# The second block's input: the first norm's tokens are transposed as they are, and the second norm's factor goes on the projections

## The reference

```python
h = _layer_norm(DEEPNORM_ALPHA * h + ffn, ln2_g, ln2_b)      # end of the first block
hn = _rmsnorm(h, attn_norm[0])                               # h * rsqrt(mean(h*h) + EPS) * g
proj = hn @ w_in                                             # lora (c_q, c_kv, k_r), qB, kB, vB
qA = _rmsnorm(c_q, g_q) @ w_uq;  kv = _rmsnorm(c_kv, g_kv) @ w_ukv
oA = mla(qA with rotated q_rope, k_nope with rotated k_r, vA);  oB = dilated(qB, kB, vB)
h = h + concat(oA, oB) @ w_out
```

## Time and profile before

| | |
|---|---|
| median of 3 runs | 1423.23 us (1423.0 to 1424.0) |
| profiled execution, own time | 1423.59 us |
| its span | 1421.4 us |
| mean granted TensorE clock | 0.995 |
| PE busy | 1385.8 us, 97% |
| DVE busy | 698.3 us, 49% |
| ACT busy | 546.9 us, 38% |

### The profile page before, as it was taken

The page is one execution under the profiler, slowest core; times in us unless marked ns, Lnnn a source line. Parts: engine busy times, 40 slices in busy tenths (PEclk is TensorE's granted clock), DMA queues, the critical chain, the costliest instruction groups (busy, mean ns, idle before and its releaser), DMA issues.

```text
span 1421.4 us, 25839 instructions
## 1 busy us (share of the span) xinstructions
PE 1385.8 (97%) x11120; PEld 1132.7 (80%) x11120; DVE 698.3 (49%) x1102; ACT 546.9 (38%) x867; POOL 18.6 (1%) x15
## 2 busy tenths in 40 slices
PE   7999999999999999999999999999999998999998
PEld 5999999979766566656666568889999986899997
DVE  6866896547611111111111157865555667755555
ACT  4555774344211111111111144763344366633343
POOL 0000004000000000000000000000000000000000
PEclk9999999999999999999999999999999999999999
DMA  9534434018899999999999981335444621454420
GB/s 388 237 120 178 178 135 165 15 48 363 330 397 426 424 427 425 424 426 426 425 426 426 426 354 59 131 133 217 178 177 172 255 106 45 171 197 180 177 89 30
DMA packets 31089, 351.99 MB, mean 248 GB/s; under 512 B 3088, under 2 KB 3344, under 8 KB 4880
## 3 DMA queue, kind: packets, MB, share of 16 engines
q1 hardware_dynamic: 30704, 349.24, 61.0%
q10 hardware_dynamic: 288, 1.31, 0.2%
HBM read 349.49 MB, written 1.05 MB: 247 GB/s over the span
## 4 chain that ended last, share of the span: by engine, by line
PE 90%; DVE 5%; ACT 3%; issue 1%; DMA 0%; DVEq 0%; ACTq 0%
PE psum L442 88%; PE psum L548 2%; ACT pages L1269 1%; PE psum L871 1%; DVE slot_lo L1873 1%; DVE tiny L1821 0%; ACT w_hi L1293 0%; DVE pages L2055 0%; DMA pages<-in_x 0%; ACT mix_hi L1293 0%; DVE pages L2492 0%; DVE pages L2540 0%; DVE pages L2538 0%; DVE pages L1843 0%; ACT tiny L1269 0%
## 5 line engine op out<-in xcount | busy, mean ns | idle before, releaser
L442 PE MATMUL psum<-pages 64*64 64x64 f32 (+9 forms) x3184 | 299.5, 305 | 8.9 <-issue 2.7
L442 PEld LDWEIGHTS psum<-pages 128*64 128x64 f32 (+3 forms) x3184 | 215.2, 151 | 78.9 <-issue 43.0
L442 PE MATMUL psum<-ring,pages 128*64 128x256 f32 (+1 forms) x1652 | 223.2, 424 | 0.9 <-ACT pages L1531 0.9
L442 PE MATMUL psum<-x_hi,gu_hi 128*128 128x256 f32 x704 | 199.8, 284 | 0.1
L442 PE MATMUL psum<-x_hi,gu_lo 128*128 128x256 f32 x704 | 199.2, 283 | 0.0
L442 PE MATMUL psum<-x_lo,gu_hi 128*128 128x256 f32 x704 | 199.2, 283 | 0.0
L442 PEld LDWEIGHTS psum<-ring,pages 128*64 128x64 f32 x1652 | 117.1, 137 | 92.1 <-issue 42.6
L442 PEld LDWEIGHTS psum<-x_hi,gu_hi 128*128 128x128 f32 x704 | 134.9, 192 | 2.7 <-issue 0.6
L442 PEld LDWEIGHTS psum<-x_lo,gu_hi 128*128 128x128 f32 x704 | 134.9, 192 | 1.6
L442 PEld LDWEIGHTS psum<-x_hi,gu_lo 128*128 128x128 f32 x704 | 134.9, 192 | 0.0
L1873 DVE TENSOR_TENSOR slot_lo<-ring,mix_hi 128x2048 fp32r<-128x2048 f32 x44 | 100.8, 2290 | 55.7 <-ACT mix_hi L1293 55.6
(11 more groups left out here) (234 smaller groups left out, 2052.0 us busy)
## 6 DMA issues: line engine op xcount, KB each, us to landing
ring<-in_w SPq DMA_DIRECT2D x62, 2048.0 KB, 23.9
pages<-in_w SPq DMA_DIRECT2D x34, 2048.0 KB, 24.3
ring<-in_ffn SPq DMA_DIRECT2D x44, 1536.0 KB, 6.4
ring<-in_w_in SPq DMA_DIRECT2D x16, 2048.0 KB, 8.6
ring<-in_e_in SPq DMA_DIRECT2D x3, 2048.0 KB, 30.6
ring<-in_w_pa SPq DMA_DIRECT2D x2, 2048.0 KB, 7.7
ring<-in_w_pb SPq DMA_DIRECT2D x2, 2048.0 KB, 8.0
ring<-in_w_o SPq DMA_DIRECT2D x2, 2048.0 KB, 7.4
```

The lines of the kernel that those rows point to most:

```text
L442: return pe.matmul(o, lhsT, rhs, start=start, stop=stop, skip_group_check=True)
```

## The change

The tokens of the layer norm are transposed as they are, as soon as two pieces are there. `rstd` is put on what the projections give: on lora by DVE (a second factor in the two scalings, a product in place of the copy) and in ACT's sums of squares (a scale), on qB and kB by DVE with a row of factors that PE spreads into PSUM, on vB by ACT with a column. The evacuations of qB0, kB0, qB1 and kB1 move from ACT to DVE. The 14 short products go. The split of the first weights moves behind the second low part.

```diff
@@ PE
-            for n in range(14):
-                mm(psum[:, 0, 0:P], ident, ones, True, True)
...
-            spread("att0", tm(11))
+            for i in range(4):
+                if i % 2 == 0:
+                    pe.wait_ge(*V("ln2_tokens", i + 2))
+                transposes(f"att0_T{i}", [tm(0)[:, b, k * P:(k + 1) * P] for k in (2 * i, 2 * i + 1) for b in range(NB)])
             x = {"hi": page_part[8], "lo": page_part[1]}
             project_tokens("lora", [("e_in", 0)], (page_high[5], page_high[7]), x, spread_done("att0"), LORA)
+            pe.wait_ge(*V("norm_rstd", 4))
+            o = take("att0_rows")
+            for b in range(NB):
+                last = mm(o[:, b * P:(b + 1) * P], rstd[:, b:b + 1].broadcast_to([P, P]), ident, True, True)
+            give(last, "att0_rows")
             split_unit("qB0", ("e_in", 1), 0, page_high[11], x)
@@ ACT
+            spread_high("att0", page_part[8], "att0")
             token_rstd(3, lambda n: V("ln2_tokens", n + 1))
-            spread_high("att0", page_part[8], "att0")
             split_high(MIXER_PAIRS + 4)
+            act_e.wait_ge(*V("norm_rstd", 4))
             for b in range(NB):
                 v = await_full(act_e, f"lora{b}")
-                act(..., v[:, 0:MLA_Q], ACT.Square, accum_out=lora_sums[:, b:b + 1])
+                act(..., v[:, 0:MLA_Q], ACT.Square, scale=rstd[:, b:b + 1], accum_out=lora_sums[:, b:b + 1])
...
-                act(page(4)[...][:, :, c * T:(c + 1) * T], v.rearrange("p (b c) -> p b c", b=NB), ACT.Copy, f"vB{c}")
+                for b in range(NB):
+                    act(page(4)[...], v[:, b * T:(b + 1) * T], ACT.Copy, f"vB{c}" if b else None, scale=rstd[:, b:b + 1])
...
-            heads_out("qB", 0, 0, DIL_SCALE)
...
-            keys_out(0)
...
-                if i == 1:
-                    heads_out("qB", 1, 0, DIL_SCALE)
-                elif i == 3:
-                    keys_out(1)
@@ DVE
-            split_low(MIXER_PAIRS + 1)
...
-            token_scale("att0", 3)
-            spread_low("att0", page_part[8], page_part[1], "att0")
+            spread_low("att0", page_part[8], page_part[1], "att0", (0, 1))
+            split_low(MIXER_PAIRS + 1)
+            spread_low("att0", page_part[8], page_part[1], "att0", (2, 3))
             split_low(MIXER_PAIRS + 4)
...
-                do(ve.tensor_scalar(lora[:, b, 0:MLA_Q], v[:, 0:MLA_Q], lora_rstd[:, b:b + 1], None, ALU.mult))
+                do(ve.tensor_scalar(lora[:, b, 0:MLA_Q], v[:, 0:MLA_Q], lora_rstd[:, b:b + 1], rstd[:, b:b + 1], ALU.mult, ALU.mult))
...
-                do(ve.tensor_copy(lora[:, b, MLA_Q + MLA_KV:LORA], v[:, MLA_Q + MLA_KV:LORA]), f"lora{b}")
+                do(ve.tensor_scalar(lora[:, b, MLA_Q + MLA_KV:LORA], v[:, MLA_Q + MLA_KV:LORA], rstd[:, b:b + 1], None, ALU.mult),
+                   f"lora{b}")
                 settle()
                 ve.sem_inc(S("lora_tokens"), 1)
+            v = await_full(ve, "att0_rows")
+            do(ve.tensor_copy(even_rstd_rows, v[:, 0:T]), "att0_rows")
+            settle()
+            def heads_out(part, n, off, scale):
+                v = await_full(ve, f"{part}{n}")
+                do(ve.scalar_tensor_tensor(two_heads(page(5)[:, off + n * 512:off + (n + 1) * 512]), two_heads(v), scale,
+                                           bc(even_rstd_rows, 1, [P, 2, T]), ALU.mult, ALU.mult), f"{part}{n}")
+            def keys_out(n):
+                heads_out("kB", n, D, 1.0)
+                settle()
+                ve.sem_inc(S("qkB_ready"), 1)
...
             ve.sem_inc(S("kA_ready"), 1)
+            heads_out("qB", 0, 0, DIL_SCALE)
             for n in range(HEADS // 2):
                 v = await_full(ve, f"qA{n}")
...
             split_low(MIXER_PAIRS + 5)
+            keys_out(0)
             def early_lows(i):
+                if i == 1:
+                    heads_out("qB", 1, 0, DIL_SCALE)
+                elif i == 3:
+                    keys_out(1)
```

More of the change, by code:

```diff
@@ L300, in build @@
         rstd_rows = page(2)[:, 3 * T:4 * T]
+        even_rstd_rows = page(9)[:, 7 * T:8 * T]
         odd_rstd_rows = page(11)[:, 2 * T:3 * T]
@@ L1671, in ffn_inputs @@
                 token_rstd(4 + 2 * layer, ready, (2, 3))
+            spread_high("att0", page_part[8], "att0")
             token_rstd(3, lambda n: V("ln2_tokens", n + 1))
-            spread_high("att0", page_part[8], "att0")
             split_high(MIXER_PAIRS + 4)
+            act_e.wait_ge(*V("norm_rstd", 4))
             for b in range(NB):
                 v = await_full(act_e, f"lora{b}")
-                act(page(2)[:, b * HALF:b * HALF + MLA_Q], v[:, 0:MLA_Q], ACT.Square, accum_out=lora_sums[:, b:b + 1])
-                act(page(2)[:, b * HALF + MLA_Q:b * HALF + MLA_Q + MLA_KV], v[:, MLA_Q:MLA_Q + MLA_KV], ACT.Square, accum_out=lora_sums[:, 2 + b:3 + b])
+                act(page(2)[:, b * HALF:b * HALF + MLA_Q], v[:, 0:MLA_Q], ACT.Square, scale=rstd[:, b:b + 1],
+                    accum_out=lora_sums[:, b:b + 1])
+                act(page(2)[:, b * HALF + MLA_Q:b * HALF + MLA_Q + MLA_KV], v[:, MLA_Q:MLA_Q + MLA_KV], ACT.Square,
+                    scale=rstd[:, b:b + 1], accum_out=lora_sums[:, 2 + b:3 + b])
             st.settle()
@@ L1684, in _ @@
             act(lora_rstd, lora_rstd, ACT.Exp, "lora_rstd", scale=-0.5)
[L1686 to L1695, removed]
             def values_out(c):
                 v = await_full(act_e, f"vB{c}")
-                act(page(4)[:, D:2 * D].rearrange("p (b c) -> p b c", b=NB)[:, :, c * T:(c + 1) * T],
-                    v.rearrange("p (b c) -> p b c", b=NB), ACT.Copy, f"vB{c}")
+                for b in range(NB):
+                    act(page(4)[:, D + b * 512 + c * T:D + b * 512 + (c + 1) * T], v[:, b * T:(b + 1) * T], ACT.Copy,
+                        f"vB{c}" if b else None, scale=rstd[:, b:b + 1])
                 st.settle()
                 act_e.sem_inc(S("vB_ready"), 1)
-            heads_out("qB", 0, 0, DIL_SCALE)
             v = await_full(act_e, "cqT")
@@ L1738, in early_behind @@
             def early_behind(i):
-                if i == 1:
-                    heads_out("qB", 1, 0, DIL_SCALE)
-                elif i == 3:
-                    keys_out(1)
-                elif i in (2, 4):
+                if i in (2, 4):
                     split_high(MIXER_PAIRS + 6 + i // 2)
@@ L2514, in _ @@
                 v = await_full(ve, f"lora{b}")
-                do(ve.tensor_scalar(lora[:, b, 0:MLA_Q], v[:, 0:MLA_Q], lora_rstd[:, b:b + 1], None, ALU.mult))
-                do(ve.tensor_scalar(lora[:, b, MLA_Q:MLA_Q + MLA_KV], v[:, MLA_Q:MLA_Q + MLA_KV], lora_rstd[:, 2 + b:3 + b], None,
-                                    ALU.mult))
-                do(ve.tensor_copy(lora[:, b, MLA_Q + MLA_KV:LORA], v[:, MLA_Q + MLA_KV:LORA]), f"lora{b}")
+                do(ve.tensor_scalar(lora[:, b, 0:MLA_Q], v[:, 0:MLA_Q], lora_rstd[:, b:b + 1], rstd[:, b:b + 1], ALU.mult, ALU.mult))
+                do(ve.tensor_scalar(lora[:, b, MLA_Q:MLA_Q + MLA_KV], v[:, MLA_Q:MLA_Q + MLA_KV], lora_rstd[:, 2 + b:3 + b],
+                                    rstd[:, b:b + 1], ALU.mult, ALU.mult))
+                do(ve.tensor_scalar(lora[:, b, MLA_Q + MLA_KV:LORA], v[:, MLA_Q + MLA_KV:LORA], rstd[:, b:b + 1], None, ALU.mult),
+                   f"lora{b}")
                 settle()
                 ve.sem_inc(S("lora_tokens"), 1)
+            two_heads = lambda ap: ap.rearrange("p (a t) -> p a t", a=2)
+            v = await_full(ve, "att0_rows")
[9 more added lines that the diff above has]
+                ve.sem_inc(S("qkB_ready"), 1)
             ve.wait_ge(*V("attn_tables", 16))
@@ L2533, in _ @@
             ve.sem_inc(S("kA_ready"), 1)
-            two_heads = lambda ap: ap.rearrange("p (a t) -> p a t", a=2)
+            heads_out("qB", 0, 0, DIL_SCALE)
             for n in range(HEADS // 2):
```

## The result

The changed kernel took 1428.88 us in the median of twelve executions (1425.79 to 1430.82), the kernel before 1423.38 us beside it. The ratio is 1.0036 with a 95% interval from 1.0029 to 1.0043: slower by 5.1 us (4.1 to 6.1); the medians themselves lie 5.5 apart. The profiled execution took 1425.93 us (span 1424.1, granted clock 0.997) and is the second fastest of the twelve; eight of them have a clock of 0.993 or less.

The account below looks back on a forecast made before the run. PE was taken as the bound, holding 90% of the chain, so only its standstills count. -3.4 + 0.5 + 3.4 + 0.95 + 0.8 = +2.25, +3.85 with the clock: 1423.23 + 3.85 = 1427.1 us, range 1423.3 to 1428.9.

Parts of the forecast that it names:

- Front: Second block's first norm: transposes start at the second piece, so lora starts sooner; gain 3.4 us (2.9 to 4.05).
- Lora: Lora's scaling on DVE and ACT's sums of squares take longer with the factor; +0.5 us (0 to 0.8).
- qB0: Before qA0, PE waits until DVE, queued behind kr's rotation, empties qB0's bank; first turn +3.4 us (3.0 to 4.0).
- Bank turn: First scores wait for the shared bank: kB0 in the even layer +0.95 us, vS in the odd layer +0.8.
- Rest: qB1 and kB1 on DVE in the attention's rounds: counted as nothing; 0.1 to 0.7 us with cover gone.
- Clock: PE's 3.6 us hole before qA0 drops the granted clock, so qA0 takes 3.7 us, not 1.97; +1.6 (0 to 2.7).
- the first (the clock holds): At the hole before qA0 the clock stays up, as at 918; +2.25, 1425.5 us; chance 0.22.
- The second rival (DVE not late): PSUM is emptied before PE needs the banks, decided at qA0: 1420.3 us, or 1422.1 with smaller waits; chance 0.15.
- The third: Clock also falls at the front, only transposes running before lora: 1.7 us more, 1428.8 us; chance 0.05.
- The fourth (no sooner start): Lora doesn't start sooner, low parts waiting behind other DVE work: 3.4 us more, 1430.5 us; chance 0.03.

Follow-up runs that it names:

- Front and lora alone: Changed kernel, but qB, kB and vB leave PSUM on ACT as in the kernel before, no factor rows spread: 1420.80 us, ratio 0.9976 to the kernel before.
- the hole filled: Changed kernel plus three products nobody reads on PE between kr and qA0: 1425.95 us, ratio 1.0015 to the kernel before.
- the loop alone: Kernel before with one call moved: DVE empties qB0 behind kr's rotation, times its constant, without the factor: 1429.11 us, ratio 1.0040.
- the turn alone: Kernel before with one turn of the four PSUM banks skipped ahead of qB0, nothing else: 1425.23 us, ratio 1.0010.
- one call earlier: Changed kernel with DVE emptying qB0 ahead of its wait for kr: 1421.79 us, ratio 0.9988 to the kernel before.
- both edits: Changed kernel with qB0 emptied ahead of DVE's wait for kr and the factor's rows in bank 4, outside the turn: 1420.56 us, ratio 0.9980 to the kernel before.

## Why the prediction was right, and where its sizes were off

The forecast was 1427.1 us, slower, with a range to 1428.9; it came out slower at 1428.88, at the very edge of that range, so that the range just held is luck. Every step was found at its place; two sizes were too small.

- *Front*, -3.4. ACT's split of the next weights, which stands behind lora's high parts, moved from 850.43 to 846.44, of which 0.66 was there at the end of the experts already, ahead of the change (the granted clock fell near 377 in the profile before and not in this one): -3.3. The wait before the second pass was 0.45 (0.65 in the prediction). Front and lora alone gave -2.9 of the -2.9 that these two terms make. Right.
- *Lora*, +0.5. Measured 0.52 from there to the transposes. Two columns cost 544 against 480 ns, as read from the earlier trace rows; ACT's squares with a scale took 463 ns in place of the 374 of the earlier trace rows.
- *qB0*, +3.4. The mechanism was right to the bank; the size is 3.9. From the transposes to the first turn it was 860.97 - 856.58 = 4.39 before, and with the hole filled, at full clock, 862.10 - 853.83 = 8.27. What is over lies in the last hand-over: DVE took up the first turn 0.48 us behind the end of ACT's copy (861.91 + 0.60 to 862.99 in the chain above), where 0.15 was counted. It is not part of the loop. With the loop alone it is 0.11, and 865.85 - 856.89 = 8.96, less the 1.11 by which ACT's copy came later behind qA0's start than in the earlier trace rows, less 4.39, leaves 3.5: the forecast's size. It is 0.17 in the profiles of the kernel before, front alone and the turn alone, but 0.48 to 0.53 in all ten in which DVE also multiplies by the rows of factors, one call earlier and both edits among them. The chain calls 0.44 of it "issue", so it is no wait that the profile shows; its cause stays open.
- *Bank turn*, +0.95 and +0.8. Measured 0.94 and 0.83 between the profiles; alone +1.6 in the medians. Right.
- *Rest*, nothing. In the attention it is at most 0.1 us in the traces, and the run with both edits lies within 0.3 us of the front alone by the medians, although it has these products. Right, but for the hand-over of 0.4 just named, for which the forecast has no term.
- *Clock*, +1.6. At qA0 it was 3.59 - 1.97 = 1.62, as forecast, with the fall beginning at 858.15 (857 to 862 in the prediction). This is the term that was too small for the usual execution: only one fall, at one place, was counted, and three of five profiles have a second one in the attention, worth 1.6, which the first profile lacks. Against the profile before, the five steps make -3.3 + 0.5 + 3.9 + 1.6 + 0.9 + 0.8 = +4.4 in place; the first profile gives back 0.66 that it was ahead, 0.84 in the odd layer, where the clock fell once and in the profile before twice, and 0.3 ahead of that layer, where the wait of 0.31 is gone. So that pair alone, 2.7 us apart in the span and 2.3 in its own time, would have made the change look half as bad as it is.

Of the rivals, the first (the clock holds) rested on the 1.00 at 918. That was one execution's luck: with the same wait of 2 us the clock did fall there in seven of the fourteen profiles at hand. The fall at 1186, on which the forecast's term rests, was luck as well: behind that wait of 2.3 us it came in six of the fourteen. What held was the argument that this hole is longer. Its price was sound: the filled hole is this case made by hand, +2.3 where +2.25 was forecast. The second rival (DVE not late) was out as DVE's order said, and one call earlier makes it true: then the change is faster. The third, that the clock falls at the front because only transposes run, didn't happen: the granted clock was 1.00 in 832 to 840 after, with a front of transposes from 832.68 on. By the Trainium skill's "TensorE: Matmul & The Clock Gate", Part 4 (PE-mode transpose), transposes don't count as PE activity in the way that other products do; this trace gives that no support, though idle products run up to 832.61 and lora starts at 835.34, so that the stretch with transposes alone is short. The fourth (no sooner start) fell with the front.

## What to carry to other kernels

When an evacuation moves to another engine, its price is not its duration but its place in that engine's queue: 0.69 us of work behind a wait cost 5.5 us, and nothing that the times can tell ahead of that wait. Any extra `take` from a rotating set of banks renames all that follow, so look at which result shares a bank with the next product that PE is waiting to start. And a hole on PE is priced twice, once as a wait and once in the clock of what follows; read that from several executions, as one profile can lie at either end.

## What was unexpected of the hardware

- The granted clock's falls lasted 3.41 or 6.83 us (but for the one at the kernel's end), and the same program has them at different places from one execution to the next: at the same wait of 2 us near 918 to 925 it fell in seven of fourteen profiles, at the wait of 2.3 us near 1186 in six, and at the open hole of 3.7 us in seven of seven.
- A stretch that fell early in the hole, 1.4 to 2.0 us before the first product, stayed low for 6.83 us (three profiles); where it fell 0.14 us before or later, for 3.41 (four).
- Three products that nobody reads, 2.84 us of a 3.7 us hole, kept the clock at 1.00 and were worth 1.6 us at qA0 without making anything wait.
- DVE took up the first turn of qA 0.48 to 0.53 us behind ACT's copy in ten profiles and 0.11 to 0.17 in four; the ten are those of kernels with the products by rows of factors, wherever qB0 was emptied. Why isn't shown.
